# Reciprocal square roots of two and four columns: Newton steps on VectorE, or one power on GpSimd

## What is computed

```
h   = rms_norm(x, norm_mix)              # x / sqrt(mean(x^2) + 1e-6) * gain
qkv = h @ w_in                           # 16 heads of 64
q, k: rms_norm per head, rotary          # 4 differential, 6 dilated, 6 block-sparse heads
x  += mix(attention heads) @ w_out
x  += cross_attention(rms_norm(x), rms_norm(mem))   # 4 heads; q and k rms_norm per head
x  += (silu(h2 @ w_gate) * (h2 @ w_up)) @ w_down    # h2 = rms_norm(x, norm_ffn), width 2816
```

## Time and profile before

| | |
|---|---|
| median of 3 runs | 820.12 us (820.0 to 820.19) |
| profiled execution | 817.26 us, of which the span of the trace is 815.4 us |
| TensorE busy | 740.9 us, 91% of the span |
| VectorE busy | 509.2 us, 62% |
| ScalarE busy | 355.5 us, 44% |
| GpSimd busy | 114.4 us, 14% |
| chain that ended last | TensorE 69%, VectorE 16%, ScalarE 8% |
| mean granted TensorE clock | 0.943 of full speed |

### The profile page before, as it was taken

The page is one execution under the profiler, slowest core; times in us unless marked ns, Lnnn a source line. Parts: engine busy times, 40 slices in busy tenths (PEclk is TensorE's granted clock), DMA queues, the critical chain, the costliest instruction groups (busy, mean ns, idle before and its releaser), DMA issues.

```text
span 815.4 us, 11864 instructions
## 1 busy us (share of the span) xinstructions
PE 740.9 (91%) x4476; PEld 649.1 (80%) x4476; DVE 509.2 (62%) x930; ACT 355.5 (44%) x516; POOL 114.4 (14%) x88
## 2 busy tenths in 40 slices
PE   4967979988799999999989899798988999999997
PEld 3846758767689999999968667676877999999996
DVE  4866695727775565655567857755548555566554
ACT  5733745615443343433427464563444343343431
POOL 5502020013420000000133302001333000000000
PEclk9978989989789999999999999899958999999999
DMA  8934313133336755777448531321414377755751
GB/s 285 347 107 156 139 68 104 53 104 104 103 95 173 197 154 157 211 204 200 154 156 290 198 106 53 104 88 68 122 54 135 104 202 208 201 161 154 202 158 51
DMA packets 122158, 120.84 MB, mean 148 GB/s; under 512 B 2928, under 2 KB 95232, under 8 KB 122128
## 3 DMA queue, kind: packets, MB, share of 16 engines
q1 hardware_dynamic: 119744, 113.26, 45.5%
q0 software_dynamic: 1664, 5.86, 2.3%
q10 hardware_dynamic: 720, 1.33, 0.5%
HBM read 119.39 MB, written 1.05 MB: 148 GB/s over the span
## 4 chain that ended last, share of the span: by engine, by line
PE 69%; DVE 16%; ACT 8%; issue 3%; POOL 2%; DMA 1%; SPq 0%; DVEq 0%; ACTq 0%
PE ps L1565 29%; PE ps L1255 14%; PE ps L1580 5%; PE ps L1581 5%; PE ps L1582 5%; DVE wlo L762 3%; ACT whi L514 2%; ACT sq L588 2%; DVE ny L774 2%; PE ps L1223 2%; PE ps L1322 2%; PE ps L1516 1%; DVE sq L948 1%; DMA raw<-in_w_in 1%; DVE xn L790 1%
## 5 line engine op out<-in xcount | busy, mean ns | idle before, releaser
L762 DVE TENSOR_TENSOR wlo<-raw,whi 128x2048 fp32r<-128x2048 f32 x94 | 219.3, 2355 | 35.5 <-ACT whi L514 35.4
L514 ACT ACTIVATE whi<-raw 128x2048 fp32r<-128x2048 f32 (+1 forms) x108 | 200.6, 1873 | 25.3 <-PE ps L1255 18.8
L726 ACT ACTIVATE qkv<-qkv 128x256 f32<-128x256 f32 x44 | 18.4, 418 | 234.7 <-DVE qkv L1141 234.7
L440 POOL TENSOR_TENSOR wlo<-raw,whi 128x2048 fp32r<-128x2048 f32 (+1 forms) x14 | 56.3, 4023 | 365.2 <-ACT whi L514 365.2
L1565 PE MATMUL ps<-thi,whi 128*128 128x256 f32 x704 | 101.3, 288 | 1.4 <-ACT thi L519 1.4
L1565 PE MATMUL ps<-thi,wlo 128*128 128x256 f32 x704 | 101.0, 287 | 0.0
L1565 PEld LDWEIGHTS ps<-thi,whi 128*128 128x128 f32 x704 | 95.2, 195 | 5.2 <-ACT thi L519 2.0
L1565 PE MATMUL ps<-tlo,whi 128*128 128x256 f32 x704 | 99.3, 284 | 0.0
L1565 PEld LDWEIGHTS ps<-thi,wlo 128*128 128x128 f32 x704 | 93.1, 197 | 0.0
L1565 PEld LDWEIGHTS ps<-tlo,whi 128*128 128x128 f32 x704 | 91.5, 193 | 0.0
L1255 PE MATMUL ps<-wlo,thi 128*128 128x512 f32 x224 | 66.7, 422 | 13.6 <-DVE wlo L762 13.6
(11 more groups left out here) (173 smaller groups left out, 948.3 us busy)
## 6 DMA issues: line engine op xcount, KB each, us to landing
raw<-in_w_gate_up SPq DMA_DIRECT2D x88, 512.0 KB, 5.3
raw<-in_w_in SPq DMA_DIRECT2D x24, 1024.0 KB, 6.5
raw<-in_w_down SPq DMA_DIRECT2D x22, 1024.0 KB, 5.0
raw<-in_w_out SPq DMA_DIRECT2D x8, 1024.0 KB, 5.0
raw<-in_w_mkv SPq DMA_DIRECT2D x4, 1024.0 KB, 5.3
xn<-in_mem POOLq DMA_DIRECT2D x2, 1024.0 KB, 6.1
raw<-in_w_mq SPq DMA_DIRECT2D x4, 512.0 KB, 3.4
raw<-in_w_mo SPq DMA_DIRECT2D x2, 1024.0 KB, 4.9
```

The source lines that it names most:

```text
L440: pool.tensor_tensor(wlo[s][:, 0:n], raw[s][:, 0:n], whi[s][:, 0:n].bitcast(F32), ALU.subtract)\
L514: act.activation(whi[s][:, 0:n], raw[s][:, 0:n], ACT.Copy).then_inc(hi_done[s].sem, 1)
L726: act.activation(silu_g[b], gate_n[b], ACT.Silu).then_inc(silu_done.sem, 1)
L762: dve.tensor_tensor(wlo[s][:], raw[s][:], whi[s][:].bitcast(F32), ALU.subtract)\
```

## The change

All roots of two and four columns go to GpSimd, as one `tensor_tensor` with the operation `pow` and a tile of -0.5. VectorE computes the mean plus epsilon, raises `root_in`, and its next instruction waits for `root_out`. The GpSimd list gets one such `pow` for each root at a fixed place. Roots of 8, 32 and 48 columns stay as they were.

```
+        minus_half = sb("minus_half", [P, 4])
+            def root(n):                                   # GpSimd
+                roots[0] += 1
+                pool.wait_ge(root_in.sem, roots[0])
+                pool.tensor_tensor(ny[:, 0:n], nv[:, 0:n], minus_half[:, 0:n], ALU.pow).then_inc(root_out.sem, 1)
...
                     .then_inc(s_gain.sem, 16)              # after the load of g_mem
+                root(T)
...
                 if layer == 0:
                     pool.wait_ge(s_memss.sem, 1)
+                    root(T)
                 pool.tensor_tensor(xn[:], xn[:], g_mem[:]...
...
-                for u in (U_MO, U_FFN, U_FFN + 1, U_FFN + 2):
-                    split_lo(layer, u)
+                split_lo(layer, U_MO)
+                for t in range(T):
+                    root(MEM_HEADS)
+                split_lo(layer, U_FFN)
+                split_lo(layer, U_FFN + 1)
+                root(T)
+                split_lo(layer, U_FFN + 2)
...
+            def power(ins):                                # VectorE
+                roots[0] += 1
+                ins.then_inc(root_in.sem, 1)
+                dve.wait_ge(root_out.sem, roots[0])
...
-                mean_eps(nv[:, 0:T], ss[:], D)
-                rsqrt(T)
+                power(dve.tensor_scalar(nv[:, 0:T], ss[:], 1.0 / D, EPS, ALU.mult, ALU.add))
                 dve.tensor_copy(rs[:, n, :], ny[:, 0:T]).then_inc(rs_ready.sem, 1)
...
+            dve.memset(minus_half[:], -0.5)
             dve.memset(ones[:], 1.0).then_inc(s_ones.sem, 1)
...
-                        mean_eps(nv[:, 0:T], mem_ss[:], D)
-                        rsqrt(T)
+                        power(dve.tensor_scalar(nv[:, 0:T], mem_ss[:], 1.0 / D, EPS, ALU.mult, ALU.add))
                         dve.tensor_copy(mem_r[:], ny[:, 0:T]).then_inc(s_memr.sem, 1)
...
-                    link(dve.tensor_scalar(nv[:, 0:4], nh[:, 0:4], 1.0 / HD, var_x[:, t:t + 1], ALU.mult, ALU.add))
-                    rsqrt(4)
+                    power(dve.tensor_scalar(nv[:, 0:4], nh[:, 0:4], 1.0 / HD, var_x[:, t:t + 1], ALU.mult, ALU.add))
```

More of the change, by code:

```diff
@@ L285, in trunk @@
         down_even = signal("down_even", PAIRS)
+        root_in = signal("root_in")
+        root_out = signal("root_out")
         dve_chain = signal("dve_chain")
@@ L441, in split_lo @@
                     .then_inc(lo_done[s].sem, 1)
+            roots = [0]
+            def root(n):
+                roots[0] += 1
+                pool.wait_ge(root_in.sem, roots[0])
+                pool.tensor_tensor(ny[:, 0:n], nv[:, 0:n], minus_half[:, 0:n], ALU.pow).then_inc(root_out.sem, 1)
+            pool.wait_ge(s_ones.sem, 1)
             for layer in range(DEPTH):
@@ L777, in mean_eps @@
                 link(dve.tensor_scalar(dst, sums, 1.0 / width, EPS, ALU.mult, ALU.add))
+            roots = [0]
+            def power(ins):
+                roots[0] += 1
+                ins.then_inc(root_in.sem, 1)
+                dve.wait_ge(root_out.sem, roots[0])
             def roots_of_x(layer, n, norm):
                 dve.wait_ge(ss_done.sem, ss_done.at(layer, norm + 1))
-                mean_eps(nv[:, 0:T], ss[:], D)
-                rsqrt(T)
+                power(dve.tensor_scalar(nv[:, 0:T], ss[:], 1.0 / D, EPS, ALU.mult, ALU.add))
                 dve.tensor_copy(rs[:, n, :], ny[:, 0:T]).then_inc(rs_ready.sem, 1)
```

## The result

The changed kernel took 810.23 us (median of 4 runs, 808.96 to 812.48) beside 820.06 us of the kernel before (4 runs, 817.14 to 820.19): a ratio of 0.9892, 95% interval 0.986 to 0.9923. Timed again (`after_timed`, 6 runs beside 19 of the kernel before), the ratio was 0.9915 (0.989 to 0.9939), 810.96 us against 817.47. That second figure, about 7 us, is the better measure: all runs of the kernel before lie between 813.6 and 820.2 us, and three of the four in the first comparison lay at the upper end, at 820.0 to 820.2.

The account below looks back on a forecast made before the run. TensorE, busy 91%, was taken as the bound, VectorE's roots costing time only where it waits. Terms 0.2 + 3.7 + 0 - 1.9 - 3.4 - 1.5 = -2.9 us gave 817.2 us from 820.12, range 811.8 to 824.5.

Parts of the forecast that it names:

- Memory rows, +3.7 us: Memory rows, layer 0: GpSimd's 128x2048 product behind the power holds VectorE, so unit 5's split comes 3.74 us later.
- VectorE gets in first: Rival at the memory rows: copy and split start before GpSimd's product; term -0.95 us, total 812.6 us; chance 0.12.
- Memory query, -1.9 us: Memory query, both layers: each qscale comes 0.95 us earlier, counted once in each layer.
- First norms, +0.2 and 0 us: First norm: layer 0's later split delays TensorE by about 0.2 us; layer 1's has 1.2 us to spare, so 0.
- Feed-forward norm, -3.4 and -1.5 us: Feed-forward norm: TensorE's idle 1.53 and 1.84 us before the row product go, plus layer 1's 1.5 us clock dip.
- The anchor: Starting time for the sum: the median of the runs shown, 820.12 us, 2.86 us above the profiled 817.26.
- A slow power: Rival: a power over 1.5 us leaves VectorE held at the feed-forward norm; 824.4 to 830.6 us; chance 0.18.
- A slow first use: Rival: the program's first power delays TensorE at the first norm by 0.7 us more, 817.9 us; chance 0.05.
- Nothing from query and clock: Rival: memory query and clock dip give no gain, leaving +0.5 us, 820.6 us; chance 0.15.

Follow-up runs that it names:

- product_first: The changed kernel with GpSimd's 128x2048 product of the memory rows ahead of their power instead of right behind it; 807.67 us, ratio 0.9879.
- mem_query: The changed kernel with powers for memory rows and memory query only, Newton steps for the first and feed-forward norms; 818.85 us, ratio 1.0009 to the kernel before.
- before_again: The kernel before, unchanged, run once more for a second profile; 818.99 us.

## Why the prediction missed

**Memory rows, +3.7 us: the mechanism right, the size near.** The product started 0.07 us ahead of the copy, which was held for 4.45 us. The split is 3.2 us later and A 3.1 us longer, as the power and the product were shorter than priced (0.69 and 4.49 us instead of 0.93 and 4.67) and the split started right at the product's end. Alone the part costs 4.3 us. "VectorE gets in first" did not happen; what it would be worth shows `product_first`.

**Memory query, -1.9 us: right in its term, one effect missing.** 0.93 us in B of each layer. Alone the powers gave 2.9 us (4.5 to 1.4); in that profile G was 1.5 us lower as well, and C and D together 1.5 us higher. Beside the feed-forward power G is low anyway.

**First norms, +0.2 and 0 us: nothing speaks against them.** In layer 0 the weights came at 28.15 with a wait of 0.31 us, against 28.00 before, and `lam_exp` 0.11 us later in the first pair; but three profiles of the changed kernel differ by 0.8 us there. In layer 1 the copy was held for 0.51 us beside a table product, and the split behind it then waited 0.29 us for ScalarE in any case.

**Feed-forward norm, -3.4 and -1.5 us: the mechanism right, the size too small. This is the step that failed.** The term was -4.9 us. Alone the power measured -6.8 us, the wait without a power -6.4 (-8.3 to -4.5), and the changed kernel against `mem_query`, which lacks this power and those of the first norms, -7.7 (about -10 to -5). Two of the three intervals take in -4.9; the three together, weighted by their widths, give -6.9, with about 1.3 to either side.

In the first pair of profiles C, F and G gave -1.46, -1.98 and -1.48 us, -4.92 against -4.9. But I priced layer 0 from one execution, in which TensorE waited 1.53 us and the clock did not dip behind the wait (D 185.12). In `before_again` it waited 1.93 us, and the clock did; these are two windows of that profile, in the form of those above:

```profile
233.00:237.00 4.00, 3.63 (x18) 3.61 (x19) 2.22 (x7) 2.01 (x2) 0.00 (x0) 0.64 0.73 260
237.00:241.00 4.00, 4.00 (x34) 4.00 (x33) 2.29 (x1) 0.22 (x1) 0.00 (x0) 0.93 0.03 8
```

So the term had put the clock dip of layer 0 at nothing, where it is 1.5 us in an execution that has it (186.59 - 185.11). C gave -1.9 us on the mean of three profiles instead of -1.53, and F gave -2.0 instead of -1.84. With the 1.5 us of G that makes -5.4 us in an execution of before without the dip of layer 0, and -6.9 in one with it. How often the kernel before has it, two profiles don't tell.

**The anchor: too high by 2.7 us.** I added to the profiled 817.26 us the 2.86 by which it lay under the median of three runs, 820.12. Later comparisons gave medians of 817.4 to 817.9 in 11 to 23 runs each. The profiled execution was typical and the three runs were high. With 817.47 the same sum would have said 814.6, and the range, moved down as much, 809.1 to 821.8, would have held the measured 810.23 and 810.96 us. That would have been luck: the change would still have been put at 2.9 us, against 7.

**What is left.** The stretches sum to 0.1 + 3.1 - 1.9 - 5.4 = -4.1 us, or -5.6 with the dip of layer 0; the second comparison says 7.0 (5.0 to 9.0). The 1.4 to 2.9 us between them stay open: E and R differ by as much between profiles of one kernel.

**The other rivals.** A slow power: 0.70 and 1.03 us excluded it, and its decision point was placed wrongly, since only the copy was counted. In its sum for 2.37 us the memory query should be +1.0, twice the loss of 0.5 named for a layer, and not +1.5; nothing measured hangs on it. A slow first use: the first power took 0.75 us, the later ones of two columns 0.69 to 0.72 in the same profile. Nothing from query and clock: B is 0.93 us shorter in each layer. The clock did not fall behind each idle time, as that rival had it (w0 of 1.53 us, D 185.12).

The Trainium skill (GPSIMD Engine Reference, "Instruction dispatch") gives about 6 us for the first call to a newly loaded kernel; the 0.75 us show no such load for a power here. A copy of 128x2 was held for 4.45 us beside GpSimd, and scalar operations as well (4.89 us for `rs_diag`, 4.47 for `qscale`). That agrees with the exclusive lock of the Trainium skill (SBUF — State Buffer, "Who interferes with whom"), for which the prediction had, as to the copy, only the page.

## What to carry to other kernels

Before moving a small operation to GpSimd, look at what stands behind it on GpSimd's list: here the next long instruction started 0.06 to 0.07 us before the VectorE instruction that waited for the result, and held it to its end. Where VectorE feeds the engine that sets the time, try first to put GpSimd's long instruction behind the last VectorE instruction of the chain, not only its first; here one such wait was worth as much as the new operation. Price a wait from more than one execution, as its length, and with it the clock behind it, differed between two executions here, and take the median of many runs as the anchor.

## What was not expected of the hardware

- A power on GpSimd takes 0.69 to 0.75 us on two columns and 1.01 to 1.05 us on four, while a 128x32 instruction, a subtraction that the prediction calls a product, took 0.25.
- VectorE's `TENSOR_SCALAR` with one input and a scalar from memory is held beside GpSimd like a copy: 4.89 us instead of 0.48.
- The loop of layer 0 takes 185.1 or 186.6 us in two executions of the kernel before, with waits of 1.53 and 1.93 us ahead of it. The stretch between the layers takes 7.6, 8.8 or 9.2 us. In the window from 412 to 425 us the granted clock was 0.87 in the profile of before and 1.00 in that of the changed kernel, but 0.87 in `after_timed` too.
